# A convolution norm's means from tiles added on VectorE, its scaling by tiles, residual rows and router sums on GpSimd, and one bank's wait moved

## What is computed

```
h = x @ w_in + b_in              # conv_a, conv_g, q, k, v, r, f_lr, gate_a, gate_b
u = depthwise_conv(conv_a * sigmoid(conv_g), 31 taps) + conv_b
u = silu(layer_norm(u, ln_g, ln_b));  y_conv = u @ w_co + b_co
merged = sigmoid(gate_a) * y_conv + sigmoid(gate_b) * y_gla     # y_gla = gla_branch(...) @ w_o
x = layer_norm(ALPHA * x + merged @ w_out + b_out, ln1_g, ln1_b)
x = layer_norm(ALPHA * x + hier_moe(x), ln2_g, ln2_b)           # 64 experts, top 1 group, top 2 in it
```

## Time and profile before

| | us |
|---|---|
| three runs, median | 1696.02 |
| lowest, highest | 1695.73, 1697.38 |
| the profiled execution | 1695.62 |
| its span in the profile | 1693.5 |
| PE busy | 1361.7 |
| DVE busy | 674.6 |
| ACT busy | 472.0 |
| POOL busy | 58.8 |

### The profile page before, as it was taken

One profiled execution on the slowest core, in us unless ns is written; L12 is line 12 of the kernel. 1 busy time (PEld: TensorE's weight loads), 2 busy tenths in 40 slices (PEclk: granted clock), 3 DMA queues, 4 the chain that ended last, 5 costly groups with the idle time before them and its releaser, 6 DMA issues.

```text
span 1693.5 us, 21308 instructions
## 1 busy us (share of the span) xinstructions
PE 1361.7 (80%) x8592; PEld 883.3 (52%) x8592; DVE 674.6 (40%) x1109; ACT 472.0 (28%) x682; POOL 58.8 (3%) x27
## 2 busy tenths in 40 slices
PE   8999999876666756666676666566799999999998
PEld 7889988522122212221221222122399999778887
DVE  4788979311001101110110011011267888655874
ACT  4464233401001001000010010010264864456653
POOL 0000000670000000000000000000000000000000
PEclk9999999889788879887887888888899999999999
DMA  8433555799999999999999999999944325475440
GB/s 345 152 144 150 213 206 247 307 432 429 431 431 431 433 431 432 432 432 431 430 433 433 432 432 431 432 430 432 421 188 150 131 73 196 174 254 176 180 174 25
DMA packets 50441, 530.79 MB, mean 313 GB/s; under 512 B 4276, under 2 KB 5556, under 8 KB 33862
## 3 DMA queue, kind: packets, MB, share of 16 engines
q1 hardware_dynamic: 50374, 529.86, 75.6%
HBM read 528.80 MB, written 1.05 MB: 313 GB/s over the span
## 4 chain that ended last, share of the span: by engine, by line
PE 53%; DMA 36%; DVE 6%; ACT 3%; issue 1%; DVEq 0%; SPq 0%; ACTq 0%
DMA shared<-in_w 36%; PE psum L1429 6%; PE psum L454 6%; PE psum L456 6%; PE psum L455 6%; PE psum L367 5%; PE psum L1450 4%; PE psum L2216 4%; PE psum L1456 3%; PE psum L1402 3%; PE psum L2217 2%; PE psum L2053 1%; DVE ring_parts L590 1%; PE psum L611 1%; PE psum L2187 1%
## 5 line engine op out<-in xcount | busy, mean ns | idle before, releaser
L1429 PE MATMUL psum<-ring,arena 128*32 128x512 f32 x992 | 142.7, 727 | 85.5 <-DMA ring<-in_w 85.4
L1429 PE MATMUL psum<-shared,arena 128*32 128x512 f32 x1040 | 147.8, 712 | 63.4 <-DMA shared<-in_w 63.3
L1659 DVE TENSOR_TENSOR shared<-shared,psum 128x512 f32<-128x512 f32 x16 | 11.0, 689 | 457.4 <-PE psum L1429 457.4
L1450 PE MATMUL psum<-shared 128*32 128x512 f32 x512 | 90.5, 843 | 67.0 <-DMA shared<-in_w 67.0
L454 PE MATMUL psum<-parts 128*128 128x256 f32 (+1 forms) x424 | 135.8, 320 | 0.7 <-DVE parts L532 0.7
L455 PE MATMUL psum<-parts 128*128 128x256 f32 (+1 forms) x424 | 134.4, 317 | 0.0
L456 PE MATMUL psum<-parts,ring_parts 128*128 128x256 f32 x464 | 131.2, 283 | 0.0
L1429 PEld LDWEIGHTS psum<-ring,arena 128*32 128x32 f32 x992 | 33.8, 130 | 182.2 <-DMA ring<-in_w 99.0
L456 PE MATMUL psum<-parts 128*128 128x256 f32 (+1 forms) x392 | 125.4, 320 | 0.0
L1429 PEld LDWEIGHTS psum<-shared,arena 128*32 128x32 f32 x1040 | 37.4, 127 | 168.3 <-issue 89.8
L454 PE MATMUL psum<-parts,ring_parts 128*128 128x256 f32 x400 | 114.8, 287 | 0.4 <-ACT shared L2250 0.4
(11 more groups left out here) (341 smaller groups left out, 2350.0 us busy)
## 6 DMA issues: line engine op xcount, KB each, us to landing
shared<-in_w SPq DMA_DIRECT2D x47, 4096.0 KB, 32.7
ring<-in_w SPq DMA_DIRECT2D x47, 4096.0 KB, 32.5
ring<-in_w_in SPq DMA_DIRECT2D x19, 2048.0 KB, 8.5
ring<-in_w_ffn_gate_up SPq DMA_DIRECT2D x11, 2048.0 KB, 8.1
ring<-in_w_gate SPq DMA_DIRECT2D x8, 2048.0 KB, 8.1
ring<-in_w_ffn_down SPq DMA_DIRECT2D x5, 2048.0 KB, 7.8
ring<-in_w_out SPq DMA_DIRECT2D x4, 2048.0 KB, 8.3
shared<-in_w SPq DMA_DIRECT2D x6, 1024.0 KB, 28.7
```

The costliest lines, as they stand in the source:

```text
L1429: m = pe.matmul(ps[slots, bank, :], V.picked[:, k, slots], w[e * len(w) // QUAD][:, e % (QUAD // len(w)), j, :], start=(k == 0), stop=(k = ...
L1450: m = pe.matmul(ps[slots, MOE_BANK["down"][c], :], V.hidden_t[:, f, slots], w(e), start=(f == 0), stop=(f == ET - 1))
```

## The change

Four parts. The means: DVE adds the 8 tiles to one (three additions of 1024, 512 and 256 columns), and PE takes one matmul instead of eight, for the mean and for the squares; subtracting and squaring go by halves. The scaling: DVE multiplies tile by tile instead of once, two of the GLA gates stand between the tiles and the others behind, and ACT makes the high part of each odd tile. The rows and the router's sums: a new program `block1_pool` does them on POOL, ahead of `moe_pool`; the sums start when the router's weights have landed. The wait for the bank of `mem_ms` moves from ahead of the places' matmuls to behind the first `pick`.

```diff
@@ block1_pe
-    pe_group(K, pe, B, "conv_mean", [K.c("j1024")] * DT, [conv[:, j, :] for j in range(DT)])
+    pe_group(K, pe, B, "conv_mean", [K.c("j1024")], [K.A(1, T)])
     pe_slab_tiles(K, pe, B, R, "go1", tiles("go", 4, 2), y, last=False)
-    pe.wait_ge(S("conv_squares"), 1)
-    pe_group(K, pe, B, "conv_var", [K.c("j1024")] * DT, [squares[:, j, :] for j in range(DT)])
+    pe.wait_ge(S("gla_conv"), GLA_CONV["squares_sum"])
+    pe_group(K, pe, B, "conv_var", [K.c("j1024")], [K.A(1, T)])
...
@@ block1_act
-    act.wait_ge(S("gla_conv"), GLA_CONV["conv_centred"])
-    L.done(act.activation(K.A(1), K.A(3), ACT.Square), S("conv_squares"))
+    for half in range(2):
+        act.wait_ge(S("gla_conv"), GLA_CONV["conv_centred"] + half)
+        L.done(act.activation(K.A(1, 1024, 1024 * half), K.A(3, 1024, 1024 * half), ACT.Square), S("conv_squares"))
...
-    act.wait_ge(S("conv_normed"), 1)
     for m in range(DT):
+        act.wait_ge(S("conv_normed"), m + 1)
...
+        if m % 2:
+            L.done(act.activation(end.cu[0][:, m, :], K.tiles(4, DT)[:, m, :], ACT.Copy), S("x_high"))
@@ block1_dve
+    add(K.A(1, 1024), K.A(3, 1024), K.A(3, 1024, 1024))
+    add(K.A(1, 512), K.A(1, 512), K.A(1, 512, 512))
+    add(K.A(1, T), K.A(1, T), K.A(1, T, T))
     dve.sem_inc(S("gla_conv"), 1)
...
-    for m in range(4):
-        gate_gla(m)
-    lows(0, 2)
+    gate_gla(0)
     b = B.wait_full(dve, "conv_mean")
...
+    gate_gla(1)
+    lows(0, 1)
+    dve_rstd(K, L, B, "conv_var", K.rstd(0))
+    for m in range(DT):
+        L.done(dve.tensor_tensor(conv[:, m, :], conv[:, m, :], K.rstd(0), ALU.mult), S("conv_normed"))
+        if m:
+            act_parts(m - 1)
+        if m in (2, 4):
+            gate_gla(m // 2 + 1)
+    act_parts(DT - 1)
+    lows(1, 2)
...
     for m in range(DT):
+        if m == 4:
+            dve.wait_ge(S("sums_rows"), ROWS_ADDED)
         gate_conv(m)
...
-            for t in range(TT):
-                L.done(dve.scalar_tensor_tensor(x1[:, t, :], x1[:, t, :], ALPHA1, K.gain("b_out"), ALU.mult, ALU.add),
-                       S("dve_steps"))
...
-    router_sums("ln1_shift", W.scaled, W.column_sums[:, NG + NE:])
...
@@ moe_pe
-    B.wait_read(pe, "mem_ms")
     pe.wait_ge(S("chosen"), 1)
...
                     if split:
                         pick(6, DT)
+                        B.wait_read(pe, "mem_ms")
                     pe.wait_ge(S("picked_act"), n + 1)
@@ new
+def block1_pool(K, pool):
+
+    S, W, V, L = K.sem, router_views(K), moe_views(K), K.line("pool", pool)
+    step, x1 = S("pool_steps"), K.tiles(1, TT, D)
+    pool.wait_ge(S("router_in"), 32)
+
+    def column_sums(name, scaled, out):
+
+        gain = last(K.v(name, 0, DT), NG + NE)
+        L.done(pool.tensor_tensor(scaled, V.w_router, gain, ALU.mult), step)
+        s = W.partial
+        L.done(pool.tensor_tensor(s[:, 0:4, :], scaled[:, 0:4, :], scaled[:, 4:DT, :], ALU.add), step)
+        L.done(pool.tensor_tensor(s[:, 0:2, :], s[:, 0:2, :], s[:, 2:4, :], ALU.add), step)
+        L.done(pool.tensor_tensor(out, s[:, 0, :], s[:, 1, :], ALU.add), S("sums_rows"))
+
+    column_sums("ln1_shift", W.scaled, W.column_sums[:, NG + NE:])
+    b_rt = W.column_sums[32:33, NG + NE:]
+    L.done(pool.tensor_tensor(b_rt, b_rt, K.A(5, NG + NE, 1610)[32:33, :], ALU.add), S("sums_rows"))
+    column_sums("ln1_gain", V.w_router, W.column_sums[:, 0:NG + NE])
+    pool.wait_ge(S("x_rows_in"), 16)
+    L.done(pool.tensor_scalar(K.A(1), K.A(1), ALPHA1, None, ALU.mult), step)
+    K.wait_gain(pool, "b_out")
+    for t in range(TT):
+        L.done(pool.tensor_tensor(x1[:, t, :], x1[:, t, :], K.gain("b_out"), ALU.add), S("sums_rows"))
+    for a in (W.group8, W.expert8):
+        L.done(pool.memset(a, NO_VALUE), S("sums_rows"))
```

More of the change, by code:

```diff
@@ L224 @@
 PLACES2 = ([2, 3, 0, 2, 3, 0, 2, 3, 0, 2, 3, 0, 2, 3, 2, 3, 0, 2, 0] + [(3, HIGHS, 2, 0)[i % 4] for i in range(17)])
-GLA_CONV = dict(gla_in=1, conv_sum=2, conv_centred=3)
+SUMS_MADE, ROWS_ADDED = 3, 3 + TT
+GLA_CONV = dict(gla_in=1, conv_sum=2, conv_centred=3, squares_sum=5)
 HGRN_END = dict(att_done=1, end_below=2, keys_end=3)
@@ L791, in block1_pe @@
         project(0, 1, i)
-    pe.wait_ge(S("router_sums"), 3)
+    pe.wait_ge(S("sums_rows"), SUMS_MADE)
     b = B.take(pe, "router_const")
@@ L1080, in block1_dve, with add @@
     dve.wait_ge(taps, CW * DT)
+    def add(out, a, b):
+        L.done(dve.tensor_tensor(out, a, b, ALU.add), S("dve_steps"))
+    add(K.A(1, 1024), K.A(3, 1024), K.A(3, 1024, 1024))
+    add(K.A(1, 512), K.A(1, 512), K.A(1, 512, 512))
+    add(K.A(1, T), K.A(1, T), K.A(1, T, T))
     dve.sem_inc(S("gla_conv"), 1)
@@ L1107, in act_parts @@
         dve.wait_ge(S("conv_act"), m + 1)
-        L.done(dve.tensor_copy(end.cu[0][:, m, :], cu[:, m, :]), S("dve_steps"))
+        if m % 2:
+            dve.wait_ge(S("x_high"), DT + m // 2 + 1)
+        else:
+            L.done(dve.tensor_copy(end.cu[0][:, m, :], cu[:, m, :]), S("dve_steps"))
         L.done(dve.tensor_tensor(end.cu[1][:, m, :], cu[:, m, :], end.cu[0][:, m, :].bitcast(F32), ALU.subtract), S("x_low"))
     def merged_low(m):
-        dve.wait_ge(S("x_high"), DT + m + 1)
+        dve.wait_ge(S("x_high"), DT + DT // 2 + m + 1)
@@ L1114, in merged_low @@
         L.done(dve.tensor_tensor(end.m8[1][:, m, :], m8[:, m, :], end.m8[0][:, m, :].bitcast(F32), ALU.subtract), S("x_low"))
[L1116 to L1120, removed]
-    for m in range(4):
-        gate_gla(m)
-    lows(0, 2)
+    gate_gla(0)
     b = B.wait_full(dve, "conv_mean")
-    L.read(dve.tensor_tensor(conv, conv, wide(ps[:, b, 0:T], DT), ALU.subtract), B, "conv_mean")
+    mean = wide(ps[:, b, 0:T], DT // 2)
@@ L1127, in block1_dve @@
+    L.done(dve.tensor_tensor(conv[:, 0:4, :], conv[:, 0:4, :], mean, ALU.subtract), S("gla_conv"))
+    L.read(dve.tensor_tensor(conv[:, 4:DT, :], conv[:, 4:DT, :], mean, ALU.subtract), B, "conv_mean")
     dve.sem_inc(S("gla_conv"), 1)
+    dve.wait_ge(S("conv_squares"), 1)
+    add(K.A(1, 512), K.A(1, 512), K.A(1, 512, 512))
+    add(K.A(1, T), K.A(1, T), K.A(1, T, T))
+    dve.wait_ge(S("conv_squares"), 2)
+    add(K.A(1, 512, 1024), K.A(1, 512, 1024), K.A(1, 512, 1536))
+    add(K.A(1, T, 1024), K.A(1, T, 1024), K.A(1, T, 1280))
@@ L1128, in block1_dve @@
+    add(K.A(1, T), K.A(1, T), K.A(1, T, 1024))
+    dve.sem_inc(S("gla_conv"), 1)
+    gate_gla(1)
[9 more added lines that the diff above has]
+    lows(1, 2)
     for m in (4, 5):
         gate_gla(m)
-    dve_rstd(K, L, B, "conv_var", K.rstd(0))
@@ L1131, in block1_dve @@
-    L.done(dve.tensor_tensor(conv, conv, wide(K.rstd(0), DT), ALU.mult), S("conv_normed"))
-    gate_gla(6)
+    lows(2, 4)
+    for m in (6, 7):
+        gate_gla(m)
     for m in range(DT):
[L1134 to L1137, removed]
+        if m == 4:
+            dve.wait_ge(S("sums_rows"), ROWS_ADDED)
         gate_conv(m)
@@ L1142, in block1_dve @@
             merged_low(m - 1)
-        if m == 3:
-            dve.wait_ge(S("x_rows_in"), 16)
-            K.wait_gain(dve, "ln1_b")
-            for t in range(TT):
-                L.done(dve.scalar_tensor_tensor(x1[:, t, :], x1[:, t, :], ALPHA1, K.gain("b_out"), ALU.mult, ALU.add),
-                       S("dve_steps"))
-            for a in (W.group8, W.expert8):
-                L.done(dve.memset(a, NO_VALUE), S("dve_steps"))
-    merged_low(DT - 1)
-    lows(10, 13)
-    dve.wait_ge(S("router_in"), 32)
-    router_sums("ln1_shift", W.scaled, W.column_sums[:, NG + NE:])
[L1155 to L1159, removed]
+    K.wait_gain(dve, "ln1_b")
+    merged_low(DT - 1)
+    lows(10, 15)
     def add_out(t, s):
@@ L1584, in router_views @@
         column_sums = K.A(5, 2 * (NG + NE), 1152)
+        partial = K.tiles(5, 4, NG + NE, 1756)
         router_const = K.A(5, 2 * (NG + NE), 1334)
@@ L2990, in _ @@
         def _(pool):
+            block1_pool(K, pool)
             moe_pool(K, pool)
```

2 lines of the change are left out of this document (1 added, 1 removed).

## The result

The changed kernel takes 1702.06 us (median of 6 runs, 1700.45 to 1704.85), the kernel before 1695.88 (median of 6) in the same set of runs. The ratio is 1.0037, with a 95% interval from 1.0024 to 1.005: slower by 6.2 us. That lies outside the range that I gave (1687.0 to 1701.0) and on the side to which I had given a chance of 0.23. The profiled execution of the changed kernel took 1704.16 us (span 1702.4), 2.1 above its median.

What follows compares the result with a forecast made beforehand. The experts' stage is bound by weights, so latency up to the first slab's use (225 to 324 us) sets the end. Terms -7.3 + 3.9 + 4.9 = +1.5 us on 1695.62 gave 1697.1, range 1687.0 to 1701.0.

Steps and rivals of the forecast that it cites:

- the side to which I had given a chance of 0.23: The whole kernel: slower by over 0.2%, above 1699.4 us; chance 0.23.
- the slower rival, with PE's clock: `go4` and `go5` at half clock after a 5.3 us wait for the mean: 1698.8 to 1700.8, or 1702; chance 0.17.
- The rows' 4.9 us: From 240.7 us, DVE's scalings and parts of tiles: POOL's reads for the rows stop DVE, 4.9 us lost.
- the 0.88 ns of one row: Line 1649 at 314.92 us: DVE lost 0.45 us for 512 POOL reads of a column, 0.88 ns each.
- the 13 us that the prediction also worked out: POOL's twelve instructions: by the skill's rule each costs DVE its full time, about 13 us, sum near +5.
- the taps' 3.9 us: Taps ahead of the mean: POOL's sums stop DVE 3.9 to 4.8 us, passed to the mean in full.
- The clock, left out of the sum: PE's clock, 0.51 from 310 to 320.5 us: left out of the sum, put into the range.
- The means and the scaling: Norm up to the tiles' parts: root taken 4.6 us earlier, last part ready 3.8 earlier.
- `co7` would end 2.8 earlier: PE behind the tiles' parts: with some 0.8 us of wait for `low(1)`, `co7` ends 2.8 earlier.
- The bank: The places' matmuls: start with `chosen`, 2.3 us earlier; 2.2 us counted as gain.
- The 0.5 for the first pick's clock: First pick of 24: shorter gaps may give back up to 2.7 us by the clock; 0.5 expected.
- The work that leaves DVE, 2.3 us: Between 265 and 287 us, rows and router's sums leave DVE, PE's low waits go: last logits another 2.3 us earlier.

Runs made afterwards that it cites:

- e4: The kernel before with POOL's program (router's sums and rows) alone, old norm and old bank wait: 1702.23 us.
- e2: The changed kernel with rows and router's sums both back on DVE, nothing of the first block on POOL: 1690.94 us.
- e1: The changed kernel with the residual rows back on DVE, the router's sums still on POOL: 1694.21 us.
- e8: The changed kernel with POOL's work on the rows cut in pieces of 256 columns (8 scalings, 8 additions): 1694.63 us.
- e11: The changed kernel with the rows on POOL in pieces of 256 columns and the router's sums back on DVE: 1691.43 us.
- e7: The changed kernel with matmuls without use on PE while it waits, 6 ahead of the mean and 14 ahead of `co0`: 1699.54 us.
- e6: The kernel before with the norm's part alone (tiles summed on DVE, scaling by tiles, high parts on ACT): 1694.59 us.
- e5: The kernel before with the moved bank wait alone: 1693.73 us.
- e10: The changed kernel with POOL's rows in pieces of 256 columns and the sums behind them, their products in two pieces: 1692.51 us.
- e3: The changed kernel with POOL's program begun only when ACT has done silu of all eight tiles, rows ahead of the sums: 1696.36 us.

## Why the prediction was wrong, point by point

**The mechanism was foreseen, its places and size were not.** The prediction had POOL's reads stop DVE and forecast +1.5; the slower rival, with PE's clock, gave +3 to +6. e4 and e2 show that POOL's program is the whole of the loss. The time fell on the end of that rival, 1702, but partly by luck: its condition was late taps and a wait of 5.3 us for the mean. The taps were not late and that wait is 2.5; what is long is the wait for the parts.

**Where on the path it went wrong.** Right behind `co7` PE starts the output projection. Its first row before and in the changed kernel, and the places' matmuls of the latter (310.98 before):

```profile
273.17 0.47 PE L454 MATMUL psum<-rowbuf_parts,arena_parts 128*128 128x512 f32 x1 [0.38 <-DVE ring_parts L590]
```

```profile
284.23 0.47 PE L455 MATMUL psum<-rowbuf_parts,arena_parts 128*128 128x512 f32 x1 [0.38 <-DVE arena_parts L1127]
...
317.17 1.33 PE L368 MATMUL psum<-shared,con 128*128 128x64 f32 x10 [0.78 <-DVEq L1635]
```

In us behind the first of the last 106 taps, from the profiles:

| | before | e2 | e1 | changed |
|---|---|---|---|---|
| output projection starts | 90.3 | 89.0 | 91.0 | 100.0 |
| places' matmuls start | 128.1 | 124.7 | 124.0 | 132.9 |
| slab is issued | 141.6 | 136.6 | 135.9 | 145.8 |

Up to the projection the terms of the sum were -2.8 + 3.9 + 4.9 = +6.0, and the profiles have +9.6. From there to the places they were -2.3 - 2.2 = -4.5, and the profiles have -4.9. So all of the miss lies ahead of the projection: -1.3 for the norm (before to e2), +2.0 for the sums (e2 to e1), +9.0 for the rows (e1 to changed).

**The rows' 4.9 us.** This is the term that failed most. The four long instructions are 8.3 us over their usual time (9.82 less 1.56); the tiles' last part comes 76.8 us behind the first tap instead of 69.1. There were two errors. I priced the scaling of 2048 columns at 1.8 us, 2048 reads at the 0.88 ns of one row, and it takes 5.38. And I let only instructions with two SBUF inputs be stopped; the casts are stopped as well. The Trainium skill ("SBUF — State Buffer", section "Who interferes with whom") names casts among those that can take both ports, and says that the one that comes first holds them for its whole instruction. The trace agrees: a cast of 0.29 took 5.20 beside the 5.37 of the scaling. For an instruction with two inputs beside the scaling it does not: that one was let in after 3.9 of the 5.4 us. I had set the rule aside for the one instruction that held DVE for 0.45 us of its 41. That price of a read was right for a power, which seems to read first and compute long behind it, and wrong for a scaling. By full times, the 13 us that the prediction also worked out, its sum would have been -7.3 + 13 = +5.7 (the prediction has "near +5"), close to the 6.2 measured.

**"The delay passes to the mean in full": the taps' 3.9 us.** This step failed too. The taps lost nothing (42.05 against 42.06 us). DVE's instructions without a gap kept POOL out, and the sums fell behind them, on the additions (3.88 instead of 2.41). What I put at 3.9 there costs 3.2 to 3.3 by e1 against e2 and e8 against e11: the size came out near by luck, since the place was another. It is also more than the 1.5 of the additions. In the profiles of the changed kernel and of e8 the clock falls behind the wait of 2.5 us, and the reciprocal starts 56.5 us behind the first tap, not 54.8 as in e1 and e7, where it doesn't fall. Additions and clock are 3.2 us together, and e8's stretch is 3.4 longer than e11's. e1's is even 0.7 shorter than e2's, at 1690.0 of span, while most of e1's runs took over 1693. That the clock falls in most runs and not in the profiled one would explain a part of that; the runs don't show it.

**The clock, left out of the sum.** It belonged in it. e7 prices it at 2.5 us, within the 1.7 to 3.7 of the rival. It fell where I had it fall only if the taps were late (behind a wait of 2.5 us), and a second time behind the wait for the parts, which I had not seen.

**The means and the scaling.** The chain up to the parts was right: the last part is ready 3.8 us earlier (65.4 behind the first tap in e2 and e6, 69.1 before). That `co7` would end 2.8 earlier was too much: it is 1.3 in e2's profile, and the norm alone is worth 1.4 in the time (e6). The expectation of e2, after the result, had put it at 1.1.

**The bank.** I had 2.2 and measured 2.2 (e5); within the noise of these runs a tenth of a microsecond is luck, but the step is confirmed: the places' matmuls start 2.3 us earlier behind the first tap in e5 than before. The 0.5 for the first pick's clock may have been too small: norm and bank together give 4.7.

**The work that leaves DVE, 2.3 us.** Behind the projection's start it came as forecast: from there to the places the changed kernel and e1 need 2.7 us less than e2. But it is paid for ahead of that. e10 has the new norm, the bank and the work on POOL in short instructions; its projection starts 2.2 us later than e2's, and at 1692.5 it is no faster than e2 at 1690.9. What leaves DVE comes back as stops.

**The way from the slab to the end.** The stretch grew by 4.2 us and the median by 6.2. In the two profiles 5.6 us of the difference are there at the slab, 6.7 when the last 4 MB have been issued and 8.9 at the end. The transfers have no new pause (1.00 in both from 1100 to 1210 us). 2.0 of the last 2.2 us arise at one place in the second block, where nothing was changed. There PE waits 2.1 us instead of 1.8 for ACT, and its clock, which stays at 1.00 before and in e4, is 0.79 from 1324 to 1332. So they belong to this one execution, which is itself 2.1 over its median. The 1.1 between the slab and the last of the weights stay open.

## What to carry to other kernels

Before work goes to GpSimd, look at what VectorE does at that very time. If VectorE is on the path there, a long GpSimd instruction on SBUF stops it for most or all of its length, casts too, and what is saved elsewhere is lost; cut to 256 columns, the same work cost VectorE 0.1 to 0.5 us at a time. Work that reads PSUM and one SBUF tile lost nothing. Test a bundle in parts: here two small gains of 4.7 us together were buried under one loss of 10.9.

## What was not expected of the hardware

- VectorE's instructions without a gap between them keep a GpSimd instruction out: one of 1.15 us took 38.18, until the taps ended.
- A long instruction and short ones of the same work differ: rows as three instructions (5.4, and 4.8 for two) stopped VectorE for 8.3 us, as sixteen (7.5 and 9.3) for 0.1 to 0.5 at a time, 1.0 in all up to the tiles' last part.
- A scaling of 2048 columns by a constant takes 5.37 us on GpSimd, more than the 4.56 of a product of two tensors of that width. The 0.40 of 256 columns there is no measure for it: that row has two constants, and the scaling by one takes 0.85 for 256 (e8).
- A cast on VectorE was held to the end of such a scaling (5.20 us, e4), an instruction with two inputs only for its first 3.9 or 4.0 us (changed kernel, e3, e7).
- PE's granted clock fell behind a wait of 2.5 us for the mean in two profiles (0.57 from 230 to 234 us in the changed kernel, 0.61 in e8) and stayed at 1.00 in another (e1) with the same wait.
